# Prompt attention of tiles five to seven with the values stationary in two 64-column groups

## The reference

```python
p_s = masked_softmax(s2 + bias_s, valid)          # selected: all earlier keys here, since 16 blocks of 64 are 1024
o_sel = einsum('btgrks,bgtksd->btgrd', p_s, gv)   # 64 value columns a head
p   = masked_softmax(s + bias, valid)             # local: the last 512 keys
o_win = einsum('bngrts,bnsgd->bntgrd', p, v)
o_a = gates[..., 0:1] * o_cmp + gates[..., 1:2] * o_sel + gates[..., 2:3] * o_win
y_a = o_a.reshape(B, T, W_A) * silu(z_a)
```

## Time and profile before

| what | value |
|---|---|
| runs | 1177.35, 1179.98, 1179.93 us; median 1179.93 |
| profiled execution | 1177.57 us, its span 1175.7 us |
| TensorE matmuls busy | 1136.6 us, 97% |
| TensorE weight loads busy | 770.2 us, 66% |
| VectorE busy | 547.9 us, 47% |
| ScalarE busy | 339.0 us, 29% |
| values L1351 | 1344 records, 173.3 us busy |
| transposes L1381 | 704 records, 116.4 us busy |

### The profile page before, as it was taken

The page is one execution under the profiler, slowest core; times in us unless marked ns, Lnnn a source line. Parts: engine busy times, 40 slices in busy tenths (PEclk is TensorE's granted clock), DMA queues, the critical chain, the costliest instruction groups (busy, mean ns, idle before and its releaser), DMA issues.

```text
span 1175.7 us, 21148 instructions
## 1 busy us (share of the span) xinstructions
PE 1136.6 (97%) x7894; PEld 770.2 (66%) x7894; DVE 547.9 (47%) x1474; ACT 339.0 (29%) x731; POOL 86.8 (7%) x209
## 2 busy tenths in 40 slices
PE   6899999899999999999999999999999999999997
PEld 2476767444454657777778787876444677777775
DVE  0211110111111357687767665653333677777773
ACT  0212110101110256555445354431111122233320
POOL 0000000000000011111010000001000200000000
PEclk8899999999999999999999999999999999999997
DMA  9764301100000441000000000001883577776770
GB/s 348 265 206 142 124 28 43 63 4 7 3 4 8 72 122 47 1 1 2 1 2 1 1 1 1 2 1 56 151 295 108 186 241 239 237 241 224 245 203 20
DMA packets 83308, 115.96 MB, mean 99 GB/s; under 512 B 30113, under 2 KB 52052, under 8 KB 82184
## 3 DMA queue, kind: packets, MB, share of 16 engines
q1 hardware_dynamic: 83208, 114.61, 31.0%
HBM read 102.31 MB, written 12.27 MB: 97 GB/s over the span
## 4 chain that ended last, share of the span: by engine, by line
PE 86%; issue 7%; DMA 2%; DVE 2%; SPq 1%; ACT 0%; POOL 0%; POOLq 0%; DVEq 0%; ACTq 0%
PE PS L516 14%; PE PS L1351 12%; PE PS L1638 9%; PE PS L1381 7%; PE PS L1331 6%; PE PS L493 5%; PE PS L461 5%; PE PS L2022 4%; PE PS L2057 3%; PE PS L1318 3%; PE PS L482 3%; DMA AR<-in_w_in 2%; PE PS L2070 2%; PE PS L1327 2%; PE PS L896 1%
## 5 line engine op out<-in xcount | busy, mean ns | idle before, releaser
L1351 PE MATMUL PS<-AR 128*128 128x65 f32 (+1 forms) x1344 | 173.3, 269 | 0.0
L1351 PEld LDWEIGHTS PS<-AR 128*128 128x128 f32 x1344 | 165.0, 192 | 0.1
L516 PE MATMUL PS<-AR 128*128 128x512 f32 (+1 forms) x384 | 161.3, 580 | 2.7 <-DVE AR L768 2.7
L1403 ACT ACTIVATE AR<-PS,SM_ 128x512 f32<-128x512 f32 (+4 forms) x304 | 131.6, 509 | 21.0 <-DVE SM_ L1475 12.9
L516 PEld LDWEIGHTS PS<-AR 128*128 128x128 f32 x384 | 73.1, 192 | 85.8 <-issue 82.1
L1381 PE MATMUL PS<-CA,AR 128*128 128x128 f32 x704 | 116.4, 281 | 0.2 <-ACT AR L1403 0.2
L1638 PE MATMUL PS<-AR 128*128 128x512 f32 x256 | 111.7, 592 | 0.0
L1413 ACT ACTIVATE AR<-PS 128x512 f32<-128x512 f32 (+1 forms) x108 | 59.1, 548 | 162.7 <-PE PS L1381 162.4
L1381 PEld LDWEIGHTS PS<-CA,AR 128*128 128x128 f32 x704 | 80.9, 148 | 30.3 <-issue 20.8
L1638 PEld LDWEIGHTS PS<-AR 128*128 128x128 f32 x256 | 47.8, 190 | 56.0 <-issue 56.0
L1331 PE MATMUL PS<-AR 64*128 64x512 f32 (+3 forms) x384 | 74.6, 494 | 4.1 <-ACT AR L1403 4.1
(11 more groups left out here) (341 smaller groups left out, 1369.1 us busy)
## 6 DMA issues: line engine op xcount, KB each, us to landing
AR<-in_cache_nsa SPq DMA_DIRECT2D x128, 256.0 KB, 4.9
AR<-in_cache_mla SPq DMA_DIRECT2D x128, 96.0 KB, 4.1
AR<-in_x_prompt SPq DMA_DIRECT2D x16, 512.0 KB, 4.6
AR<-in_w_ada SPq DMA_DIRECT2D x3, 2048.0 KB, 12.2
AR<-in_w_in SPq DMA_DIRECT2D x4, 1472.0 KB, 9.9
out<-AR SPq DMA_DIRECT2D x9, 512.0 KB, 3.5
AR<-in_w_ada SPq DMA_DIRECT2D x8, 512.0 KB, 5.9
AR<-in_w_out SPq DMA_DIRECT2D x4, 1024.0 KB, 9.6
```

The source lines that it names most:

```text
L516: mm = pe.matmul(PS[0:n, bank, 0:hi - lo], ht(j, k)[:, 0:n], w2cols(k, lo, hi), start=(k == 0), stop=(k == KT - 1))
L1351: mm = pe.matmul(out, tile, v, start=(n == 0), stop=(n == nb - 1))
L1403: act.activation(probs(u, gi, lo, hi), PSF[:, o + lo:o + hi], ACT.Exp, bias=NM[:, u % 2, gi:gi + 1], scale=-1.0).then_inc(s_exp, 1)
```

## The change

In the selected and local units of tiles 5 to 7 ("crossed" units, those whose group has `TURNS_BACK`) the operands of the value step change places: 64 columns of values are stationary, the turned probabilities' 128 columns stream, and the output, turned, goes to partitions `64 g` and up of the group g. A chunk now holds the two heads' tiles in turn (`t % 2` is the head), so that column groups alternate. On TensorE chunks go in pairs: two of transposes, then two of values. There is no column of ones; ScalarE's exponentials put their sums into `TOT`, and VectorE adds the two parts. A finished group's 256 output columns are copied to SBUF (`out_copy`, ScalarE), turned back by two transposes (`back`) into the other half of the bank, and finished one chunk later. `OT` lies where `GP`'s load used to go during attention, so that load moves behind the end of attention.

```diff
@@ -199,6 +199,7 @@
         TB = [view(49568 + 256 * n, 256) for n in range(2)]
+        OT = [view(o, 256) for o in (46496, 46752)]
         BCX = view(9216, 960).rearrange("p (g r c) -> p r g c", g=G, r=R)
@@ -254,6 +255,7 @@
         RCB, CFB = ([small(4) for _ in range(2)] for _ in range(2))
+        TOT = [small(8) for _ in range(4)]
         VCX, KCX = small(130), small(128)
@@ -1226,7 +1228,15 @@
         AV_LAG = 2
-        FIN_AT = {c: [og for og, g in enumerate(GROUPS) if CH_OF[g[3]][-1] + AV_LAG + 1 == c] for c in range(NCH + 3)}
+        TURNS_BACK = [kind in ("sel", "win") and i >= 5 for kind, i, half, last in GROUPS]
+        OUT_AT = {c: [og for og, g in enumerate(GROUPS) if TURNS_BACK[og] and CH_OF[g[3]][-1] + AV_LAG + 1 == c]
+                  for c in range(NCH + 4)}
+        FIN_AT = {c: [og for og, g in enumerate(GROUPS) if CH_OF[g[3]][-1] + AV_LAG + (2 if TURNS_BACK[og] else 1) == c]
+                  for c in range(NCH + 4)}
+
+        def crossed(u):
+
+            return TURNS_BACK[UNITS[u][6]]
@@ -1244,17 +1254,19 @@
                 return probs(u, 2 * t, 0, P)
-            return probs(u, t // nb, P * (t % nb), P * (t % nb) + P)
+            gi, n = (t % 2, t // 2) if crossed(u) else (t // nb, t % nb)
+            return probs(u, gi, P * n, P * n + P)
...
             nb = UNITS[u][5]
+            place = lambda t: (t % 2, t // 2) if crossed(u) else (t // nb, t % nb)
             if UNITS[u][0] == "cmp":
...
             if TWO[u]:
-                return EXP0[u] + max(t // nb + (2 if t % nb >= 4 else 0) for t in range(t0, t0 + nt)) + 1
-            return EXP0[u] + (t0 + nt - 1) // nb + 1
+                return EXP0[u] + max(gi + (2 if n >= 4 else 0) for gi, n in map(place, range(t0, t0 + nt))) + 1
+            return EXP0[u] + max(gi for gi, n in map(place, range(t0, t0 + nt))) + 1
@@ -1263,12 +1275,13 @@
                     nb = UNITS[v][5]
-                    first = len(PSLOTS[v]) == 2 and PSLOTS[v][0] == PSLOTS[u][n]
+                    first = len(PSLOTS[v]) == 2 and PSLOTS[v][0] == PSLOTS[u][n] and not crossed(v)
                     need = max(need, (CH_OF[v][(nb - 1) // 4] if first else CH_OF[v][-1]) + 1)
...
         s_evA, s_evD, s_av, s_fin = (sem(f"s_at_{n}") for n in ("evA", "evD", "av", "fin"))
+        s_ot, s_bt = sem("s_at_ot"), sem("s_at_bt")
         s_rc, s_cf, s_pl, s_pz = (sem(f"s_at_{n}") for n in ("rc", "cf", "pl", "pz"))
@@ -1341,13 +1354,17 @@
                     continue
-                (r, g), n = heads[t // nb], t % nb
+                (r, g), n = (heads[t % 2], t // 2) if crossed(u) else (heads[t // nb], t % nb)
                 kb = key_tiles(kind, i, k0, nb)[n]
...
                     out, v = ob[:, 129 * (r % 2):129 * (r % 2) + 129], VM[:, kb, r, :]
-                else:
+                elif not crossed(u):
                     slot = 2 * (r % 2) + g
                     out, v = ob[:, 65 * slot:65 * slot + 65], (VS1 if kind == "sel" else VW1)[:, kb, g, :]
+                else:
+                    mm = pe.matmul(ob[64 * g:64 * g + 64, P * (r % 2):P * (r % 2) + P],
+                                   (VS1 if kind == "sel" else VW1)[:, kb, g, 0:64], tile, start=(n == 0), stop=(n == nb - 1))
+                    continue
                 mm = pe.matmul(out, tile, v, start=(n == 0), stop=(n == nb - 1))
@@ -1363,6 +1380,21 @@
                 pe_values(pe, c)
+
+            def turns(u, c):
+                _, t0, nt = CHUNKS[c]
+                pe.wait_ge(s_exp, exps_for(c))
+                if c >= 2:
+                    wait_copied(pe, c - 2)
+                for t in range(t0, t0 + nt):
+                    mm = pe.transpose(PS[:, 4 + c % 2, P * (t - t0):P * (t - t0) + P], tile(u, t), ident)
+                mm.then_inc(s_trc, 1)
+
+            def back(og):
+                pe.wait_ge(s_ot, sum(TURNS_BACK[:og + 1]))
+                for n in range(2):
+                    mm = pe.transpose(PS[:, 6 + og % 2, 256 + P * n:256 + P * n + P], OT[og % 2][:, P * n:P * n + P], ident)
+                mm.then_inc(s_bt, 1)
@@ -1372,19 +1404,21 @@
                     pe_scores(pe, v)
-                for c in CH_OF[u]:
-                    _, t0, nt = CHUNKS[c]
-                    pe.wait_ge(s_exp, exps_for(c))
-                    if c >= 2:
-                        wait_copied(pe, c - 2)
-                    for t in range(t0, t0 + nt):
-                        mm = pe.transpose(PS[:, 4 + c % 2, P * (t - t0):P * (t - t0) + P],
-                                          tile(u, t), ident)
-                    mm.then_inc(s_trc, 1)
-                    if c >= AV_LAG:
-                        values(c - AV_LAG)
-            for c in range(NCH - AV_LAG, NCH):
-                values(c)
+                step = 2 if crossed(u) else 1
+                for c0 in CH_OF[u][::step]:
+                    pair = [c for c in CH_OF[u] if c0 <= c < c0 + step]
+                    for c in pair:
+                        turns(u, c)
+                    for c in pair:
+                        if c >= AV_LAG:
+                            values(c - AV_LAG)
+                        for og in OUT_AT[c]:
+                            back(og)
+            for c in range(NCH, NCH + AV_LAG + 2):
+                if c < NCH + AV_LAG:
+                    values(c - AV_LAG)
+                for og in OUT_AT[c]:
+                    back(og)
@@ -1400,8 +1434,19 @@
                         act.wait_ge(s_trc, room_for(u, gi))
+                    if crossed(u):
+                        slot = 2 * (heads[gi][0] % 2) + heads[gi][1] + (4 if lo else 0)
+                        if og >= 4:
+                            act.wait_ge(s_fin, og - 3)
+                        act.activation(probs(u, gi, lo, hi), PSF[:, o + lo:o + hi], ACT.Exp, bias=NM[:, u % 2, gi:gi + 1],
+                                       scale=-1.0, accum_out=TOT[og % 4][:, slot:slot + 1]).then_inc(s_exp, 1)
+                        continue
                     act.activation(probs(u, gi, lo, hi), PSF[:, o + lo:o + hi], ACT.Exp,
                                    bias=NM[:, u % 2, gi:gi + 1], scale=-1.0).then_inc(s_exp, 1)
+
+            def out_copy(og):
+                act.wait_ge(s_av, CH_OF[GROUPS[og][3]][-1] + 1)
+                act.activation(OT[og % 2], PS[:, 6 + og % 2, 0:256], ACT.Copy).then_inc(s_ot, 1)
@@ -1409,10 +1454,15 @@
                 for c in CH_OF[u]:
+                    for og in OUT_AT[c]:
+                        out_copy(og)
                     if BY_A[c]:
...
                     expo(u + 1)
+            for c in range(NCH, NCH + AV_LAG + 2):
+                for og in OUT_AT[c]:
+                    out_copy(og)
@@ -1487,14 +1537,17 @@
                         evac(dve, c, dve.tensor_copy, s_evD)
-            for c in range(NCH, NCH + AV_LAG + 1):
+            for c in range(NCH, NCH + AV_LAG + 2):
                 for og in FIN_AT[c]:
...
             kind, i, half, last = GROUPS[og]
-            dve.wait_ge(s_av, CH_OF[last][-1] + 1)
+            if TURNS_BACK[og]:
+                dve.wait_ge(s_bt, sum(TURNS_BACK[:og + 1]))
+            else:
+                dve.wait_ge(s_av, CH_OF[last][-1] + 1)
             ob = PS[:, 6 + og % 2, :]
@@ -1509,13 +1562,17 @@
                 return
-            o = ob[:, 0:260].rearrange("p (h c) -> p h c", h=4)
+            o = ob[:, 0:260].rearrange("p (h c) -> p h c", h=4) if not TURNS_BACK[og] else \
+                ob[:, 256:512].rearrange("p (h c) -> p h c", h=4)
             if kind == "cmp" and i == 0:
...
             else:
-                dve.reciprocal(RC, o[:, :, 64]).then_inc(s_rc, 1)
+                if TURNS_BACK[og] and TWO[last]:
+                    dve.tensor_tensor(TOT[og % 4][:, 0:4], TOT[og % 4][:, 0:4], TOT[og % 4][:, 4:8], ALU.add).then_inc(s_cl, 1)
+                    dve.wait_ge(s_cl, 2 + sum(TURNS_BACK[o] and TWO[GROUPS[o][3]] for o in range(og + 1)))
+                dve.reciprocal(RC, o[:, :, 64] if not TURNS_BACK[og] else TOT[og % 4][:, 0:4]).then_inc(s_rc, 1)
             br = ("cmp", "sel", "win").index(kind)
@@ -1576,10 +1633,10 @@
             sp_scratch(sp)
-            sp.dma_start(GP, gate_dram[8:9, :].to_broadcast([P, DM])).then_inc(s_gp, 16)
             sp.wait_ge(s_fin, NG)
...
             sp.dma_start(XO[0], x_t[1]).then_inc(s_xo[0], 16)
+            sp.dma_start(GP, gate_dram[8:9, :].to_broadcast([P, DM])).then_inc(s_gp, 16)
             sp.dma_start(GF, g_final.rearrange("(o n) -> o n", o=1).to_broadcast([P, DM])).then_inc(s_gp, 16)
```

## The result

The changed kernel took 1170.58 us in the median of five runs (1170.25 to 1173.19), the kernel before 1177.61 (1177.35 to 1179.98): a ratio of 0.9937, 95% interval 0.9922 to 0.9951, or 7.4 us less; the two medians are 7.0 us apart. The profiled executions are 1177.57 and 1170.58 us, spans 1175.7 and 1168.8. The forecast was 1173.3 and 6.6 us less.

What follows compares the result with a forecast made beforehand. TensorE was taken to bound the selected and local units: 29.1 - 12.8 - 2.6 = 13.7 us less work, half handed over to ScalarE's loop, leaving 6.6 us less, 1173.3 us (chance 0.45); 8-in-10 range 1166 to 1180.

Steps and rivals of the forecast that it cites:

- The records: Value matmuls of selected and local units, tiles 5 to 7: 0.0545 us a record instead of 0.105, 29.1 us less gross.
- The changes of grouping: TensorE going into or out of column groups: 88 more changes at 0.145 us, 12.8 us more.
- D: Rival: a change of grouping costs 0.30 us instead of 0.145, at all 88 places; 1183 us; chance 0.13 with the like.
- The loop: Scores through minima and exponentials to next scores: local units 4.2 us without a copy, 5.06 with one, against 4.51 to 4.61.
- The units: Savings summed unit by unit over tiles 5, 6 and 7: 1.2 + 2.3 + 3.1 = 6.6 us less.
- B: Rival: TensorE bounds all, exponentials don't wait for the copy as forecast; 11.4 us less, 1168.5 us; chance 0.22.
- C: Rival: hand-overs cost 0.4 us more each, or ScalarE's reads hide nothing; gain about 2 us, 1178 us; chance 0.20.
- The rest at nothing: VectorE's extra add and later finish, and SyncE's moved gate row load, cost nothing; without room the load costs some 2 us.
- The level: Starting time for the 6.6 us: 1173.3 from the median of three, chosen over 1171.0 from the profiled execution.
- the lower level only after the wait of rows 7: TensorE's clock before the change: at the lower level only after the 1.97 us wait of scores at 562.81.

## Why the prediction was right

**The records.** 0.0545 us in column groups was taken from L493. Sixteen records and one change are 1.03 us; less 0.15, 0.055 a record. Right, and for the reason given: it is the heads in turn, as the run with one head after the other shows.

**The changes of grouping.** 0.145 each was the term with the widest bounds, 0.09 to 0.30. The run without pairs gives 0.15 in runs of 4 and 8. So D falls. Their number was counted slightly low: the trace of the changed kernel has 53 visits to the column groups, which is 92 changes more than before and not 88 (14 of the exits go into scores and replace a change that was there). At 0.15 that is 13.8 us of TensorE's time where the sum had 12.8, part of it in local units, where the loop hides it; it is still the largest cost of the change. The Trainium skill says in "TensorEngine Tiling (Array Packing)", Key Properties, that changing the tiling mode drains TensorE. The trace agrees, and here one change cost 0.15 us in all.

**The loop.** 4.2 and 5.06 us were forecast for local units; 4.19 and 5.00 came. Two parts were each shown by a run of their own: the copy ahead of the exponentials (taken away: 0.57 to 0.67 less a unit; doubled: 0.28 more), the sums (0.12 without a copy, 0.18 with one). The read's 0.10 us an exponential came from a row of the decode stage with another width and held: 696.90 - 696.23 = 0.67, taken as 0.68.

**The units.** The list of the prediction gave 1.2, 2.3 and 3.1 us for the three tiles; measured are 1.3, 2.2 and 3.2. The largest miss of one unit is 0.07 us. The misses have both signs, so that the total is right to 0.1 us is in part luck. B had 11.4: its 4.7 us are what the copy on VectorE gave back, 4.4. C expected the hand-overs to cost more; TensorE isn't held by the turn back in the local unit shown, where 696.20 + 0.59 = 696.79 is the pitch of its values, and none of the twelve (L1396) carries idle time.

**The rest at nothing.** The load of the gate row moved behind 798.04 and its consumer ran at 808.06, released by TensorE as before:

```profile
798.04 0.33 SPq L1638 DMA_DIRECT2D AR<-in_x_prompt  x1
798.41 0.43 SPq L1639 DMA_DIRECT2D AR<-gate_rows  x1
...
808.06 0.69 DVE L1782 TENSOR_TENSOR AR<-PS,AR 128x512 f32<-128x512 f32 x1 [6.28 <-PE PS L1695]
```

**The level.** The 6.6 us were set against a median of three, 1179.93; with five runs that median is 1177.61, and 2.3 of the 2.7 us by which the forecast lies above the result come from that. Taken from the profiled execution it was 1171.0, against 1170.58.

## What to carry to other kernels

Price a unit of a pipeline twice: by the bound engine's work, and by the loop that hands a buffer back to it through the other engines. A cut in the first is worth only the distance to the second, and a small new instruction is priced by whose queue it stands in and what is behind it: the same copy cost 0.6 us a unit ahead of the exponentials and nothing behind the minima. Column groups pay when two of them alternate and when runs are long against 0.15 us a change.

## What the runs showed that I had not expected

In the five runs of each kernel the times fall into two clusters 2.5 us apart (1177.4 and 1179.9 before, 1170.3 and 1173.0 after); in the nine and ten runs of the kernel before that stand beside the experiments they spread more evenly, from 1176.8 to 1181.7. The traces hold something that may be behind this, and it has nothing to do with the change. It isn't shown to be the cause, since both kernels' profiled executions are of the faster cluster. Attention's first matmuls, from 428 us on, are sparse: TensorE waits for ScalarE again and again. The same stretch in the changed kernel and in the one with the copy twice, columns as in rows 2, the clock third from the end:

```profile
428.40:442.80 14.40, 12.24 (x104) 10.12 (x104) 9.47 (x51) 10.52 (x36) 0.72 (x1) 1.00 1.03 275
```

```profile
428.44:442.80 14.36, 12.94 (x74) 10.98 (x74) 7.34 (x41) 7.62 (x25) 0.00 (x0) 0.65 1.03 274
```

In the second the granted clock is at its lower level (1.2 GHz) for 10.2 us from 432.8 on, and TensorE gets through 74 instead of 104 records. From attention's first scores to those of tile 4 it is 109.7 us in the four traces without that stretch and 113.7 to 114.9 in the six with it. Four of those six in turn skip a later one of 3.4 us, near 563, behind the wait of rows 7: a unit there takes 5.04 us instead of 5.87 to 6.06. The four traces without the fall at 432 have another that the six lack: 3.4 us near 220, before attention, behind 4 us in which TensorE was busy for 1.3 (214 to 218). So the prediction was wrong that the trace of the kernel before has the lower level only after the wait of rows 7; that holds within attention alone. Why the clock falls at 432 in one execution and not in the next isn't settled here. The idle stretches of 0.5 us that the change put into the local units never moved the clock from 1.00.
